# Attention scores in whole 128-row blocks, and the softmax scaling moved from ScalarE to VectorE

## The reference, cut to what matters

```python
scores = jnp.einsum('bnqkgd,bnskd->bnkgqs', qb, kw).astype(jnp.float32) * (ATTN_HEAD_DIM ** -0.5)
rel = q_pos[:, :, None] - k_pos[:, None, :]
allowed = (rel >= 0) & (rel < WINDOW) & (k_pos[:, None, :] >= 0)      # WINDOW = 128
scores = jnp.where(allowed[None, :, None, None], scores, -jnp.inf)
probs = jax.nn.softmax(jnp.concatenate([scores, sink], axis=-1), axis=-1)[..., :-1]
out = jnp.einsum('bnkgqs,bnskd->bnqkgd', probs.astype(v.dtype), vw)
...
branch_a = jnp.einsum('bte,ed->btd', attn * jax.nn.silu(a_z), w_branch_attn)
```

## Time and profile before

| | us |
|---|---|
| median of 3 runs | 1094.35 (1093.85 to 1094.9) |
| the profiled execution, its own time | 1094.9 |
| its span in the trace | 1093.2 |
| PE busy | 1077.1 (99%) |
| DVE busy | 725.5 (66%) |
| ACT busy | 518.2 (47%) |
| POOL busy | 651.8 (60%) |
| granted TensorE clock | 0.999 of full speed |

### The profile page before, as it was taken

One profiled execution on the slowest core, in us unless ns is written; L12 is line 12 of the kernel. 1 busy time (PEld: TensorE's weight loads), 2 busy tenths in 40 slices (PEclk: granted clock), 3 DMA queues, 4 the chain that ended last, 5 costly groups with the idle time before them and its releaser, 6 DMA issues.

```text
span 1093.2 us, 16993 instructions
## 1 busy us (share of the span) xinstructions
PE 1077.1 (99%) x5631; PEld 856.4 (78%) x5631; DVE 725.5 (66%) x1116; ACT 518.2 (47%) x1252; POOL 651.8 (60%) x436
## 2 busy tenths in 40 slices
PE   6999999999999999999999999999999999999997
PEld 5887777777777778778877887788778888888886
DVE  4864785775866857566755684669569222558897
ACT  6544754746646643454445454545464311131443
POOL 2667555556555559558955797569644545447441
PEclk9999999999999999999999999999999999999999
DMA  6225133132142231114311422132209433754424
GB/s 216 64 85 101 39 105 90 39 117 68 47 145 57 68 127 39 46 42 129 95 39 40 125 87 57 38 115 87 59 11 360 160 95 134 251 173 141 167 86 146
DMA packets 113847, 111.76 MB, mean 102 GB/s; under 512 B 7340, under 2 KB 96744, under 8 KB 112760
## 3 DMA queue, kind: packets, MB, share of 16 engines
q1 hardware_dynamic: 102648, 77.08, 23.6%
q10 hardware_dynamic: 11136, 33.88, 9.2%
HBM read 84.63 MB, written 26.31 MB: 101 GB/s over the span
## 4 chain that ended last, share of the span: by engine, by line
PE 92%; POOL 2%; DMA 2%; issue 1%; ACT 1%; DVE 1%; POOLq 1%; SPq 0%; DVEq 0%; ACTq 0%
PE ps L1042 59%; PE ps L1283 16%; PE ps L951 4%; PE ps L1132 2%; PE ps L1243 2%; PE ps L1174 2%; PE ps L1181 2%; POOL ring_lo L804 1%; PE ps L1176 1%; PE ps L1231 1%; PE ps L1240 1%; DMA xs<-in_x 1%; PE ps L1236 1%; DMA w<-in_w_in 1%; PE ps L1201 1%
## 5 line engine op out<-in xcount | busy, mean ns | idle before, releaser
L804 POOL TENSOR_TENSOR ring_lo<-w,ring_hi 128x512 fp32r<-128x512 f32 x128 | 180.9, 1433 | 103.8 <-ACT ring_hi L1422 103.8
L804 POOL TENSOR_TENSOR ring_lo<-t,ring_hi 128x512 fp32r<-128x512 f32 x96 | 133.1, 1391 | 137.7 <-ACT ring_hi L1422 137.4
L1042 PE MATMUL ps<-s_hi,ring_hi 128*128 128x512 f32 x512 | 204.0, 398 | 0.0
L1042 PE MATMUL ps<-s_lo,ring_hi 128*128 128x512 f32 x512 | 200.3, 391 | 0.0
L1042 PE MATMUL ps<-s_hi,ring_lo 128*128 128x512 f32 x512 | 200.2, 391 | 0.0
L1042 PE MATMUL ps<-h_hi,ring_hi 128*128 128x512 f32 x384 | 151.8, 395 | 0.1
L1042 PE MATMUL ps<-h_lo,ring_hi 128*128 128x512 f32 x384 | 150.4, 392 | 0.0
L1042 PE MATMUL ps<-h_hi,ring_lo 128*128 128x512 f32 x384 | 150.0, 391 | 0.0
L1422 ACT ACTIVATE ring_hi<-w 128x512 fp32r<-128x512 f32 x128 | 77.3, 623 | 93.1 <-PE ps L1042 83.1
L1042 PEld LDWEIGHTS ps<-s_hi,ring_hi 128*128 128x128 f32 x512 | 96.2, 188 | 21.9 <-issue 3.3
L1042 PEld LDWEIGHTS ps<-s_hi,ring_lo 128*128 128x128 f32 x512 | 96.2, 188 | 20.3
(11 more groups left out here) (322 smaller groups left out, 2245.7 us busy)
## 6 DMA issues: line engine op xcount, KB each, us to landing
w<-in_w_in SPq DMA_DIRECT2D x128, 256.0 KB, 3.0
xs<-in_x SPq DMA_DIRECT2D x8, 512.0 KB, 8.6
ga_scratch<-ev ACTq DMA_DIRECT2D x4, 1024.0 KB, 4.2
u_scratch<-silu_z ACTq DMA_DIRECT2D x8, 512.0 KB, 3.3
c_rows<-c_scratch ACTq DMA_DIRECT2D x8, 512.0 KB, 6.1
gm_scratch<-ev ACTq DMA_DIRECT2D x4, 1024.0 KB, 4.5
w_raw<-in_w_branch_attn SPq DMA_DIRECT2D x8, 512.0 KB, 4.6
u_a_f<-u_scratch SPq DMA_DIRECT2D x4, 1024.0 KB, 9.0
```

What stands on the lines that cost most here:

```text
L804: return nc.gpsimd.tensor_tensor(flat(lo[:]), flat(raw_or_sum[:]), flat(hi[:]).bitcast(F32), ALU.subtract)
L1042: mm = nc.tensor.matmul(ps[:, bank, columns], w[:, k, :], h[:, k, columns], start=(m == 0), stop=(m == PRODUCT - 1))
```

## The change

- `scores(n)` issues one matmul for each head pair index j and each half r of the partitions, over all 128 queries and all 256 keys (128 for n = 0), instead of two halves of 64 queries with 192 keys (64 and 128 for n = 0): 4 matmuls for 8.
- The scaling of the probabilities by the inverse sums leaves ScalarE (four activations) and becomes one multiply on VectorE with a broadcast operand, placed after `combine(n)`; the semaphore `inverse_ready` goes.
- `combine` keeps the maximum with a positive sign, and needs one more small instruction to form `neg_max`; `inverse_sums` doubles the sum before the reciprocal, and `copy_v` no longer halves the values.
- The semaphore increment `passed` before the scores goes; SP has a semaphore of its own, `sp_passed`.

```diff
-                for j in range(2):
-                    for half in range(2):
-                        first = n * P if n == 0 else (n - 1) * P + 64 * half
-                        keys = 64 * (half + 1) if n == 0 else 192
-                        column = j * 2 * P + (P if n == 0 else 64 * half)
-                        for r in range(2):
-                            rows = slice(64 * r, 64 * r + 64)
-                            queries = slice(n * P + 64 * half, n * P + 64 * half + 64)
-                            mm = nc.tensor.matmul(ps[64 * half:64 * half + 64, X[r], column:column + keys],
-                                                  q_T[rows, j, queries], k_now[rows, first:first + keys],
-                                                  start=True, stop=True)
+                first = max(n - 1, 0)
+                for j in range(2):
+                    for r in range(2):
+                        rows = slice(64 * r, 64 * r + 64)
+                        o = ps[:, X[r], j * 2 * P + (P if n == 0 else 0):(j + 1) * 2 * P]
+                        mm = nc.tensor.matmul(o, q_T[rows, j, n * P:(n + 1) * P], k_now[rows, first * P:(n + 1) * P],
+                                              start=True, stop=True)
...
-                        pe.sem_inc(passed, 1)
                         scores(n).then_inc(scores_done, 1)
...
-                    if 1 <= n <= NB:
-                        earlier = probs[(n - 1) % 2]
-                        act.wait_ge(inverse_ready, NB * g + n)
-                        for h in range(GR):
-                            ins = A(earlier[:, h, :], earlier[:, h, :], ACT.Copy, scale=row_inv[:, h:h + 1])
-                        ins.then_inc(probs_ready, 1)
...
-                    V.scalar_tensor_tensor(neg_max[:], row_max[:], -HD ** -0.5, sink, ALU.mult, ALU.min)
+                    V.scalar_tensor_tensor(row_max[:], row_max[:], HD ** -0.5, sink, ALU.mult, ALU.max)
                     dve.drain()
-                    V.tensor_tensor(sink_in[:], neg_max[:], sink, ALU.subtract).then_inc(max_ready, 1)
+                    V.tensor_tensor(sink_in[:], sink, row_max[:], ALU.subtract)
+                    V.tensor_scalar(neg_max[:], row_max[:], -1.0, None, ALU.mult).then_inc(max_ready, 1)
...
-                    V.reciprocal(row_inv[:], row_inv[:]).then_inc(inverse_ready, 1)
+                    V.tensor_scalar(row_inv[:], row_inv[:], 2.0, None, ALU.mult)
+                    dve.drain()
+                    V.reciprocal(row_inv[:], row_inv[:])
+                    dve.drain()
+
+                def normalise(n):
+                    pr = probs[n % 2]
+                    V.tensor_tensor(pr[:], pr[:], row_inv[:].unsqueeze(2).to_broadcast([P, GR, P]), ALU.mult)\
+                        .then_inc(probs_ready, 1)
...
                     if n < NB:
                         combine(n)
+                    if 1 <= n <= NB:
+                        normalise(n - 1)
                     if n <= NB:
                         retire(attention_at(n, 1))
```

More of the change, by code:

```diff
@@ L399, in build @@
         probs_ready = sem("probs_ready")
-        inverse_ready = sem("inverse_ready")
         probs_turned = sem("probs_turned")
@@ L465, in build @@
         passed = sem("passed")
+        sp_passed = sem("sp_passed")
         def merged_part(half, o, j):
@@ L604, in pair_weights @@
                     sp.wait_ge(sum_made, 1)
-                sp.sem_inc(passed, 1)
+                sp.sem_inc(sp_passed, 1)
                 sp.dma_start(w11[:], w_cols[:, 0:KH, ds(c1, P)]).then_inc(w11_in, 16)
                 sp.wait_ge(w2_ready, n)
-                sp.sem_inc(passed, 1)
+                sp.sem_inc(sp_passed, 1)
                 sp.dma_start(w21[:], w_cols[:, KH:KT, ds(c1, P)]).then_inc(w21_in, 16)
                 sp.wait_ge(w7_ready, n)
-                sp.sem_inc(passed, 1)
+                sp.sem_inc(sp_passed, 1)
                 sp.dma_start(w12[:], w_cols[:, 0:KH, ds(c2, P)]).then_inc(w12_in, 16)
                 sp.wait_ge(w3_ready, n)
-                sp.sem_inc(passed, 1)
+                sp.sem_inc(sp_passed, 1)
                 sp.dma_start(w22[:], w_cols[:, KH:KT, ds(c2, P)]).then_inc(w22_in, 16)
@@ L2115, in _ @@
             dve.wait_ge(vectors_in, 16 * 3)
-            V.tensor_scalar(sink_tab[:].rearrange("p (g r j) -> p g j r", r=2, j=2),
-                            sink_raw[:].rearrange("p (g j r) -> p g j r", r=2, j=2), -1.0, None, ALU.mult)
+            V.tensor_copy(sink_tab[:].rearrange("p (g r j) -> p g j r", r=2, j=2),
+                          sink_raw[:].rearrange("p (g j r) -> p g j r", r=2, j=2))
             dve.wait_ge(g_moved, ENDS_IN)
@@ L2129, in copy_v @@
                 for b in range(2):
-                    ins = V.tensor_scalar(v_stage[n][:, :, 4 * b:4 * b + 4, :].rearrange("p r c d -> p c r d"),
-                                          ps[:, X[2 * n + b], :].rearrange("p (c r d) -> p c r d", r=2, d=HD), 0.5, None,
-                                          ALU.mult)
+                    ins = V.tensor_copy(v_stage[n][:, :, 4 * b:4 * b + 4, :].rearrange("p r c d -> p c r d"),
+                                        ps[:, X[2 * n + b], :].rearrange("p (c r d) -> p c r d", r=2, d=HD))
                 ins.then_inc(v_ready, 1)
```

## The result

The changed kernel takes 1101.46 us in the median of 4 runs (1100.76 to 1102.17), against 1094.1 (1092.86 to 1094.9). The ratio is 1.0065, with a 95% interval of 1.0053 to 1.0077: slower by 7.4 us. The forecast was 1101.3.

The account below looks back on a forecast made before the run. The prediction took PE's own stream to bound the attention stretch. Its terms 5.9 + 0.2 + 0 + 0.8 = +6.9 us on 1094.9 gave 1101.8, or 1101.3 as median; range 1098.0 to 1107.0.

Parts of the forecast that it names:

- TensorE's stream sets the time: Attention stretch, 90 to 400 us: PE waits for no other engine, so its own stream sets the time.
- +0.21 us a burst, 5.9 us: Score bursts of blocks 1 to 7 on PE: four rounds of 64 more columns, +0.21 us in each of 28 bursts.
- my upper bound from the very shape: Score burst priced from the second mixer's 64*128 passes: 1.08 us, so +0.27 a burst, 7.6 us.
- Block 0: Score bursts of block 0 on PE: 0.59 us becomes 0.65, +0.06 for 4 bursts, 0.2 us.
- Weight loads in the open: Rival, chance 0.04: score weight loads wait for their tile's passes, 0.27 us a burst on top, 7.6 us, 1108.9.
- The increment on TensorE: 0: Removing the increment of `passed` before each score burst on PE saves 0, bounds 0 and -0.3 us.
- ScalarE's relief: 0: Four activations of 0.39 us each leave ScalarE per block; mostly a longer wait for `sink_in`, worth 0 us.
- VectorE's added work, 46 us: VectorE in the attention: multiply 0.80, doubling 0.35, sign 0.30, 1.45 us a block; busy 217 to some 263 us.
- A stall of 0.8 us: PE held up by VectorE's queue for 0.2 us once in each g, bounds 0 and 7.4 us.
- the forecast's own span: Values if columns set the burst and VectorE holds, chance 0.60: 1098.6 to 1103.3 us.
- Which check is the tight one: VectorE's queue: `select` at step 8 to line 1174, margin 0.1 us; the transposes behind it, 0.3 us.
- VectorE as the bound, 0.20: Rival, chance 0.20: VectorE's queue holds PE up; half the bound gives 1104.2 us, the whole 1107.9.

Follow-up runs that it names:

- The scores alone: Kernel before with only the new scores (whole blocks, 64*128 tiles, 256 keys), scaling still on ScalarE, increment kept: 1101.49 us, ratio 1.0065.
- the 192 keys on the wide tile: Kernel before with whole-block scores on 64*128 tiles but only 192 keys, so part of the scores is left out: ratio 1.0007.
- the softmax alone: Changed kernel with the old scores (halves, 192 keys, increment before them), scaling on VectorE: 1100.49 us, ratio 1.0054.
- the one with the extra instruction before the reciprocal: Kernel before with the multiply on VectorE plus one small instruction and drain between sum and reciprocal: 1094.97 us, ratio 1.0006.
- the run with one instruction more: Changed kernel with one more 128x512 VectorE instruction per block, a maximum of the probabilities with themselves, and a drain: 1118.71 us, ratio 1.0227.
- the run with the multiply before `combine`: Changed kernel with the old scores and the multiply moved ahead of the next block's copy and maximum in VectorE's queue: 1109.28 us, ratio 1.0141.

## Why the prediction was right, and where it was not

- **TensorE's stream sets the time, and a burst is paid 32 times.** Right. The scores alone give the whole ratio of 1.0065.
- **+0.21 us a burst, 5.9 us.** The mechanism was right, the size low: 0.25 us, 7.0 us. The nearest rows gave 0.21 for the columns (0.22 measured). I left out what comes with the wider tile, 0.03, although my upper bound from the very shape was 1.08 against the 1.06 measured. Block 0: +0.05 for +0.06.
- **Weight loads in the open.** Out, by the 192 keys on the wide tile (0.85 us). Its price was also too high: a load of 128 columns lasts 187 ns and one of 64 lasts 133, so the difference is under a third of it and not "at least half". The rule in Part 3 of TensorE: Matmul & The Clock Gate in the Trainium skill, that loads hide only beneath matmuls of other row groups, would have made that burst longer; the measurement decides. The same section also says that a load can be pulled ahead into a background weight buffer; I had left that out, and the 0.85 us do not speak against it.
- **The increment on TensorE: 0. ScalarE's relief: 0.** Both right. The gap stays at 0.32 us; ScalarE's wait grew to 55.6 us.
- **VectorE's added work, 46 us.** Of the prices, the multiply was 0.93 for 0.80, the doubling 0.64 for 0.35, the sign 0.20 for 0.30. The sum is 57 us, but busy time grew from 217 to only 248, 79% of the stretch where I had said 80 to 85. Of the 25 us between, 19 are waits that other small instructions no longer have, and 6 are rows of neighbouring instructions that overlap. One wait behind GpSimd is paid once, by whichever instruction comes first; I had added it to each. So the lag came out smaller than I worked it out.
- **A stall of 0.8 us.** It was 0. (The upper end of the forecast's own span also adds up to 1103.1, not 1103.3.) The two errors, 1.1 us too little on the bursts and 0.8 too much here, nearly cancel, so the hit is better than its working.
- **Which check is the tight one.** Here a step was wrong. I followed `select` to line 1174 at step 9 and the last block's transposes. The transposes at step 8 read the multiply of block 6, which stands behind `combine(7)` in VectorE's queue, and that is where the softmax alone waits the longest. I never worked out that margin; it is 1.3 us in each g of the changed kernel, and 0.1 in the last g of the one with the extra instruction before the reciprocal.
- **VectorE as the bound, 0.20.** Not in the changed kernel, but it was nearer than its trace shows. I took the 0.6 us that the longer bursts give to VectorE as a small correction. It is the reason why the small delays of each g are gone: with the old bursts the same softmax loses 6 us. Whether it is also the whole reason in the last g is not shown. There the softmax alone lost 2.1 us in two meetings with GpSimd, more than the margin of 1.3, and the changed kernel's multiply at the same place met none (0.68 us); how the two queues happen to lie against each other is in part luck. What the forecast got right by adding two terms is really the later of two queues: measured apart, 7.1 us on TensorE (1.0065) and 5.9 on VectorE (1.0054).

What stays open is how much of the time past VectorE's limit is its own work and how much its meetings with GpSimd; no run separates them. TensorE's lower clock can be read from the traces: it is about 1.6 us each in the softmax alone and in the run with one instruction more, both times behind the single longest wait, and nothing in the run with the multiply before `combine`, where the clock stayed at 1.00 through ten waits of up to 1.8 us.

## What to carry to other kernels

When a change does two things, measure them apart before blaming one: here each alone costs what both cost, and taking either one back alone gains nothing or a tenth of a percent. If one engine's stream sets the time, price a matmul by moving columns times rounds, with tiles side by side counted as one, and cut masked columns by finer tiles; the point at which issuing the many passes would set the burst was not met here, with 32 of them in 0.71 us. For an engine in its idle time, work out the margin at each instruction that the bound engine reads, in queue order, with waits for a shared resource counted once, and treat a margin shorter than one such wait, 1.1 us here, as none. A list of waits shows where to look, not what is lost: compare the starts of the same instructions in both kernels.

## What the runs showed of the hardware

- Bursts of 32, 16 and 8 float32 passes on 64*32, 64*64 and 64*128 tiles cost what four rounds of their columns cost, as if eight, four and two passes ran side by side: 0.71 and 0.81 us for 160 and 192 columns on the first two, 1.03 for 256 on 64*64, and 0.85 and 1.06 for 192 and 256 on 64*128. 32 passes with their loads fit in 0.71 us, 0.022 us each.
- A VectorE instruction with two SBUF operands loses up to 1.1 us to a GpSimd instruction that started 0.08 us before it. A small `tensor_scalar` with one operand is stretched too: 0.17 us at best and 1.30 at worst in the softmax alone. `reciprocal` is not: 177 to 180 ns in all 32.
- In the softmax alone TensorE's loads waited 2.4 us and its matmuls stood idle for 1.93; about 3.4 us at the lower clock followed, some 1.6 us of loss on top.
